# When x is loaded, who copies the vectors, and the order of small products at the start of a two-block transformer kernel

## The reference, cut to what matters

```python
c_act = silu(c)                                    # 1 x 1024
mod = c_act @ w_ada[0] + b_ada[0]                  # 1024 x 6144: 24 MB of weights
sh_m, sc_m, gt_m, sh_f, sc_f, gt_f = split(mod, 6)
h = rms_norm(x, g_mix) * (1 + sc_m) + sh_m         # x: 256 x 1024
proj = h @ w_in[0]                                 # 1024 x 5120
```

## Time and profile before

| what | value |
|---|---|
| median of 3 runs | 1467.77 us (1467.56 to 1468.4) |
| span of the profiled execution, first to last instruction | 1467.5 us |
| TensorE busy | 1409.0 us, 96% of the span |
| VectorE, ScalarE, GpSimd busy | 894.0, 736.9, 84.6 us |
| mean granted TensorE clock | 0.990 |
| VectorE idle before its first instruction, until e0 has landed | 10.47 us |
| first TensorE product of x with a weight | at 28.98 us |

### The profile page before, as it was taken

The page is one execution under the profiler, slowest core; times in us unless marked ns, Lnnn a source line. Parts: engine busy times, 40 slices in busy tenths (PEclk is TensorE's granted clock), DMA queues, the critical chain, the costliest instruction groups (busy, mean ns, idle before and its releaser), DMA issues.

```text
span 1467.5 us, 18626 instructions
## 1 busy us (share of the span) xinstructions
PE 1409.0 (96%) x7111; PEld 1174.9 (80%) x7111; DVE 894.0 (61%) x1124; ACT 736.9 (50%) x1013; POOL 84.6 (6%) x133
## 2 busy tenths in 40 slices
PE   4999998999999999999899999999999999999998
PEld 4878876899987888877687888878888778788886
DVE  5577785788776545468856554466545444664553
ACT  4447745645546443357556444355443567464342
POOL 3011100000000000031300000000000100000000
PEclk9999999999999999999989999999999999999999
DMA  9787654476744655444335765537655463466550
GB/s 352 272 304 237 212 168 163 151 251 230 254 148 159 229 188 185 148 152 140 99 121 178 232 200 186 187 106 260 194 184 189 128 209 101 159 229 194 180 172 29
DMA packets 177448, 274.31 MB, mean 187 GB/s; under 512 B 6450, under 2 KB 120882, under 8 KB 177362
## 3 DMA queue, kind: packets, MB, share of 16 engines
q1 hardware_dynamic: 170656, 250.87, 51.8%
q0 software_dynamic: 5552, 20.20, 4.3%
q10 hardware_dynamic: 1153, 2.07, 0.4%
HBM read 272.05 MB, written 1.06 MB: 186 GB/s over the span
## 4 chain that ended last, share of the span: by engine, by line
PE 47%; DVE 2%; issue 1%; ACT 1%; POOL 0%; POOLq 0%; DVEq 0%; ACTq 0%
PE psum L2410 14%; PE psum L2412 14%; PE psum L2411 14%; DVE w_lo L2026 1%; PE psum L2638 1%; PE psum L2507 1%; PE psum L2576 1%; ACT w_hi L1830 0%; PE psum L2591 0%; PE psum L2592 0%; PE psum L2588 0%; DVE scr L2372 0%; PE psum L2561 0%; PE psum L2560 0%; PE psum L2522 0%
## 5 line engine op out<-in xcount | busy, mean ns | idle before, releaser
L2026 DVE TENSOR_TENSOR w_lo<-raw,w_hi 128x2048 fp32r<-128x2048 f32 (+1 forms) x158 | 359.9, 2280 | 191.4 <-ACT w_hi L1830 190.6
L2410 PE MATMUL psum<-w_hi,hT_hi 128*128 128x512 f32 x912 | 366.3, 402 | 15.4 <-DVE w_lo L2026 8.5
L1830 ACT ACTIVATE w_hi<-raw 128x2048 fp32r<-128x2048 f32 (+1 forms) x158 | 299.8, 1900 | 125.6 <-PE psum L2412 79.1
L2412 PE MATMUL psum<-w_hi,hT_lo 128*128 128x512 f32 x912 | 356.9, 391 | 0.0
L2411 PE MATMUL psum<-w_lo,hT_hi 128*128 128x512 f32 x912 | 356.5, 391 | 0.0
L2410 PEld LDWEIGHTS psum<-w_hi,hT_hi 128*128 128x128 f32 x912 | 172.6, 189 | 56.9 <-issue 18.1
L2412 PEld LDWEIGHTS psum<-w_hi,hT_lo 128*128 128x128 f32 x912 | 172.3, 189 | 37.2
L2411 PEld LDWEIGHTS psum<-w_lo,hT_hi 128*128 128x128 f32 x912 | 172.7, 189 | 33.3 <-issue 0.5
L2026 DVE TENSOR_TENSOR lo_qk<-raw,hi_qk 128x2048 fp32r<-128x2048 f32 (+1 forms) x35 | 79.2, 2264 | 39.9 <-ACT hi_qk L1830 39.8
L2026 DVE TENSOR_TENSOR lo_at<-raw,hi_at 128x2048 fp32r<-128x2048 f32 x35 | 80.2, 2290 | 34.8 <-ACT hi_at L1830 34.8
L2410 PE MATMUL psum<-w_hi,hc_hi 128*128 128x512 f32 x256 | 100.4, 392 | 0.7 <-issue 0.5
(11 more groups left out here) (228 smaller groups left out, 2342.3 us busy)
## 6 DMA issues: line engine op xcount, KB each, us to landing
raw<-in_ffn_wg_dram SPq DMA_DIRECT2D x88, 512.0 KB, 3.9
raw<-in_ffn_wu_dram SPq DMA_DIRECT2D x88, 512.0 KB, 4.9
raw<-in_ffn_wd_dram SPq DMA_DIRECT2D x44, 1024.0 KB, 4.9
raw<-in_w_up_dram SPq DMA_DIRECT2D x44, 512.0 KB, 5.0
raw<-in_w_in_dram SPq DMA_DIRECT2D x19, 1024.0 KB, 7.5
ada_raw<-in_w_ada_dram POOLq DMA_DIRECT2D x24, 512.0 KB, 5.2
raw<-in_even_w_in_dram SPq DMA_DIRECT2D x12, 1024.0 KB, 5.0
raw<-in_odd_w_in_dram SPq DMA_DIRECT2D x12, 1024.0 KB, 5.2
```

The source lines that it names most:

```text
L1830: nc.scalar.activation(hi_of(s), raw_of(s), ACT.Copy)\
L2026: nc.vector.tensor_tensor(lo_of(s), raw_of(s), hi_of(s).bitcast(F32), ALU.subtract).then_inc(lo_ready, 1)
L2410: nc.tensor.matmul(o, a_hi, b_hi, start=start, stop=False)
L2412: return nc.tensor.matmul(o, a_lo, b_hi, start=False, stop=stop)
```

## The change

1. The load of x on GpSimd's queue waits until e0, the first megabyte of modulation rows, has landed.
2. The four copies of the transposed vectors are made by ScalarE and no longer by VectorE. VectorE still waits for them.
3. The `var` step stands behind ada(2,0) in the plan, where it stood ahead of it.
4. adasum(1) stands ahead of the first tiles of va and so ahead of ada(3,1); va runs two tiles there (it was one) and two (it was three) after the transposes.

```diff
     vector_uses = [pl.use(b) for b in (4, 5, 6, 7)]
     pl.add("vectors", uses=vector_uses)
-    st = x_stats([("x_loaded", 16)] * TT)
+    st = tile_stat()
+    squared = x_squares(st, (0, 1), [("x_loaded", 16)] * TT)
     pl.add("warm", use=vector_uses[3], times=8)
     ada(2, 0)
+    var(st, (0, 1), squared, False, EPS)
     pl.add("normalise", st=st, half=0)
...
     ada(3, 0)
-    product_step("proj", va[1][0], ks=(0,), inc=None)
+    adasum(1, shared=shared)
+    product_step("proj", va[1][0], ks=(0, 1), inc=None)
     shared3 = shared_ada(3, 3, 3)
-    adasum(1, shared=shared)
     adasum(3, shared=shared3)
     rest = turn_early(G, ("scr_ready", v), ("mod", 1), ("mod", 0), 4, (2, 3))
-    product_step("proj", va[1][0], ks=(1, 2, 3))
+    product_step("proj", va[1][0], ks=(2, 3))
...
+            pool.wait_ge(early_landed[0], 16)
             pool.dma_start(X[:, :, :], x[0].rearrange("(t p) d -> p t d", p=P)).then_inc(x_loaded, 16)
...
+                elif kind == "vectors":
+                    for use, dst, w in ((a["uses"][0], cols[:, :], NV), (a["uses"][1], ada_b[:, :], 48),
+                                        (a["uses"][2], conv_c[:, 0:88], 88), (a["uses"][3], conv_c[:, 88:176], 88)):
+                        wait_ready(act, use)
+                        nc.scalar.activation(dst, psum[:, use.bank, 0:w], ACT.Copy).then_inc(psum_read[use.bank], 1)
...
                 if kind == "vectors":
 
-                    for use, dst, w in ((a["uses"][0], cols[:, :], NV), (a["uses"][1], ada_b[:, :], 48),
-                                        (a["uses"][2], conv_c[:, 0:88], 88), (a["uses"][3], conv_c[:, 88:176], 88)):
-                        wait_ready(dve, use)
-                        ins = nc.vector.tensor_copy(dst, psum[:, use.bank, 0:w])
-                        ins.then_inc(psum_read[use.bank], 1)
                     for use in a["uses"]:
                         wait_read(dve, use)
```

## The result

The changed kernel took 1477.37 us in the median of 4 runs (1474.71 to 1479.07) against 1468.09 for the kernel before: the ratio is 1.0057, 95% interval 1.0043 to 1.0071. That is 9.3 us slower, where 4.9 slower was forecast with a range that ended at 1476.0. The ratio is not the quotient of the two medians, which would be 1.0063; by the ratio the change costs 8.4 us. Two repeats on two chips (e11 and e12) gave 1.0059 (1.0041 to 1.0077) and 1.0060 (1.0043 to 1.0078). The profiled execution spans 1477.3 us, 9.8 more than the one of before.

A forecast was written before the change was run, and what follows sets the result against it. TensorE's in-order list was taken to bound the kernel, so a later start shifts the rest: +1.5 (late transposes) +3.1 (half clock) +0.3 (second half) = +4.9 us, giving 1472.7 us, range 1466.5 to 1476.0.

The forecast's parts named there:

- x behind e0, first part: Start: without x beside it e0 lands at 7.6 and VectorE starts 2.8 us sooner, a head start then lost.
- When x lands: Start: x, issued at 7.6, needs 8.2 us as before (7.4 if less crowded) and lands at 15.5.
- The term +1.5: Variance to transposes: transposes at 21.5 against 20.04, +1.5 us, between +0.7 and +2.5.
- Half clock in the small products: Four groups of small products on TensorE run at half clock after idle time: +3.1 us, between 0 and 3.7.
- The second half: Around va and the later adasums: TensorE gains 0.4, waits 3 us for unit 4: +0.3, between -0.4 and +1.5.
- Nothing gives it back, and nothing adds: After the start: everything keeps its order, so the sum of +4.9 us stays to the end.
- The base: Whole kernel: profiled span 1467.5 becomes 1472.4; the median, 0.3 above the span, becomes 1472.7.
- A: Rival, chance 0.25: the small products run at full clock, only the late x costs, +1.5 us, 1469.5.
- B: Rival, chance 0.10: not slower, full clock carries into the first products and the second half gains: -0.4 us, 1467.4.
- C: Rival, chance 0.07: truly faster, e2 lands 2.8 us sooner and VectorE's head start carries through, 1465.
- D: Rival, chance 0.05: the change does nothing, x issued later but the rest absorbs it, 1467.8.

The follow-up runs named there:

- e11: The changed kernel run again, unchanged, against the kernel before: 1477.16 us, ratio 1.0059 (1.0041 to 1.0077), first product at 34.2.
- e12: The changed kernel once more, on another chip, against the kernel before: 1477.59 us, ratio 1.0060 (1.0043 to 1.0078).
- e1: The kernel before with only the wait of GpSimd's x load on e0 added: ratio 1.0033 (1.0022 to 1.0043), first product at 34.4.
- e3: The changed kernel with 44 warming products where it has 8: ratio to the kernel before 1.0027 (1.0018 to 1.0036), first product at 31.6.
- e4: The changed kernel with the move of adasum(1) and the va tiles undone: 1475.2 us, ratio to the kernel before 1.0043 (1.0027 to 1.0060).
- e13: The changed kernel with the move of adasum(1) and the va tiles undone, run again: 1475.58 us, ratio to the kernel before 1.0045 (1.0030 to 1.0060).
- e2: The kernel before with only adasum(1) moved ahead of two tiles of va: ratio 1.0006 (0.9995 to 1.0017).
- e5: The changed kernel without the wait of the x load: 1476.85 us against 1470.48 before, ratio 1.0034 (1.0022 to 1.0047).
- e8: The kernel before with ScalarE's vector copies, squares and variance between ada(0,0) and ada(0,1), and unit 1's split behind modfinal: ratio 0.9985 (0.9974 to 0.9997).
- e10: The kernel before with only the variance moved behind ada(2,0): ratio 1.0034 (1.0022 to 1.0047), first product at 34.2.
- e14: A second run of the kernel before with ScalarE's vector copies, variance between ada(0,0) and ada(0,1), unit 1's split behind modfinal: ratio 0.9983 (0.9972 to 0.9994).
- e6: The kernel before with only the four vector copies moved to ScalarE: ratio 1.0009 (0.9998 to 1.0020), transposes at 18.4, first product at 30.1.

## Why the prediction was wrong

The mechanism came as forecast: a late x, then small products at half clock, then a wait for unit 4. What failed is the size of three terms. The landing of x was taken too early (+1.5 became +2.9 at the transposes), part 4 was put at +0.3 and cost 2.0, and what comes behind the start was put at nothing and added about 1.

*x behind e0, first part: right in the number, not in the working.* e0 at 7.6, VectorE 2.8 us sooner, worth nothing, since VectorE then waits for e2 and for the squares. But the terms given for it, 1.05 MB and the identity at 0.39 MB per us from 3.5, make 6.4 and not 7.6. Nor did e0 have the queue to itself: by 7.6 SyncE's queue had moved some 1.5 MB, so e1 came beside e0. That the number fits is in part luck.

*When x lands: mis-sized.* The step took 15.5 and got 17.5. The issue was at 7.9, not 7.6, and landing took 9.6 us, not 8.2 or less: 8.9 to 10.0 in seven profiles with the wait (changed, e1, e3, e4, e11 to e13), 8.2 to 9.1 in the eight where x was issued at 1.4 (before, e2, e5 to e8, e10, e14). The 7.4 in the step's lower bound is in no run. The step assumed that a queue alone among fewer would start no later. It started later, at some 4 us behind the issue instead of 2; why is open. e2 profited: 14.4 instead of 15.9. So the variance waited for the squares (20.0) and not for ada(2,0) (18.8): +1.2. The prediction had named this case, x slower and e2 sooner, and gave it no term. GpSimd's power then took 1.06 us instead of 0.79, as in e10 but not in e1: +0.3. The term +1.5 measured +2.9.

*Half clock in the small products: right.* +3.1 was forecast, 12.1 minus 8.9 us from transposes to first product is +3.1. (Its row, 0.68 for four fifths of a group, gives 0.85 a group rather than the 0.78 taken, 3.4 in all.) The Trainium skill, "TensorE: Matmul & The Clock Gate", Part 1, What's actually happening, says that activity releases the throttle; e3 agrees, with nothing but added activity and 3.5 us won at the first product. Whether transposes keep the clock up less than products do, on which the prediction leant too, no run tests by itself. What the prediction did not see is how little is needed: the idle time behind the warming was 8.2 us, but gaps of 2.2 and 2.3 us cost as much or nearly so (3.1 in e10, 2.7 in e6). Hence parts 1 and 3 don't add up; each alone makes the first product 5.5 and 5.2 us late.

*The second half: mechanism right, size wrong.* The wait of TensorE for unit 4 came with 3.07 us where 3 was worked out, and TensorE saved nothing by being early. The term took +0.3, a middle between -0.4 and +1.5. The runs show 2.0 and 2.2 us for part 4: in the changed kernel, e5, e11 and e12 the clock fell in that wait or within 1.5 us behind it. In e3 it did not, and e2, alone, lost 0.9, which may be nothing.

*Nothing gives it back, and nothing adds: wrong by about 1 us.* 6.1 at the start and 2.0 for part 4 leave 1.2 of the 9.3. The same sum leaves 1.4 in e11 and 0.7 in e12. In the profiled run it is the two stretches at half clock near 247 and 445. All three profiles of the changed kernel have both, and those of before, e2 and e8 have neither; but e14, which is faster than before, has both as well, and e3 and e13 have the first alone. No edit was shown to cause them, so this part stays open.

*The base.* The span 0.3 us under the median was read as one execution. In the later runs the time stands 1.7 to 2.6 us above the span of the profiled execution, so that of before was itself probably some 1.5 us slower than the median. Differences between profiled runs carry that.

*Rivals.* A (small products at full), B (not slower), C (faster) and D (nothing) all fall at the groups of 1.7 to 1.85 us. C wanted e2 2.8 us sooner; it came 1.5 sooner, and the late x took that away.

## What to carry to other kernels

A warming is worth what follows it without a gap: work that comes early on TensorE because its wait was removed can leave a hole before the next, and the hole can cost more than was gained, as in e6 (1.6 us won at the transposes, 2.7 lost behind them). Before a wait is moved, read which of the engine's neighbours in time keep its clock up; here moving one step of 0.17 us cost 5 us at the first product. Where the transfers were full, as here, putting one load behind another only swapped which was late; ask for the one that the last wait needs.

## What was not expected of the hardware

- The clock column read 1.00 for the first 15 to 40 us of most profiles, while eight transposes took 1.97 us there (e1, e10) and 1.04 at full clock: in this column the time before the first change is not a measurement.
- A gap of 2.2 us behind 3.8 us of warming left all four groups of small products at 1.7 to 1.85 us (e10); the same groups right behind warming and transposes took 1.0 (before). In e6 a gap of 2.3 us came behind a warming in which the clock had already risen, and the groups were as slow.
- A half-clock stretch of 3.4 us cost 1.6 us when it fell behind the wait for unit 4 (changed, e5, e11); where it fell ahead of unit 4 (e13), TensorE still waited 0.4 us for that unit.
- A load of 1 MB issued by GpSimd at 7.3 to 7.9 us, beside a queue that already kept the transfers full, landed 8.9 to 10.0 us later; issued at 1.4 us it took 8.2 to 9.1.
